# Laying V out by rows behind the weight tiles of the first three stages instead of behind the tiles of U

## What is computed

```python
z = x @ w_in                                   # split among the conv group and the GLA group
mix = concat(conv_mixer(...), gla_mixer(...)) @ w_out
x = layer_norm(ALPHA * x + mix, ln1_g, ln1_b)
# PEER: 8 heads, 128 x 128 product keys, top 16, N_EXPERTS = 16384
q = x @ w_query;  s = q . sub_keys;  ids, gates = top-k of top-k
h = gelu(einsum('td,thkd->thk', x, u_table[ids]))
y = einsum('thk,thkd->td', gates * h, v_table[ids])
x = layer_norm(ALPHA * x + y, ln2_g, ln2_b)
```

## Time and profile before

| | |
|---|---|
| Median of 3 runs | 3986.06 us (3980.82 to 3989.38) |
| The profiled execution's own time | 3983.18 us |
| Its span, first to last instruction | 3981.4 us |
| TensorE busy | 3814.9 us, 96% of the span |
| VectorE, ScalarE, GpSimd busy | 2230.6, 939.1, 1821.2 us |
| Moved by DMA | 751.76 MB |
| Mean granted TensorE clock | 0.972 of full speed |

### The profile page before, as it was taken

The page is one execution under the profiler, slowest core; times in us unless marked ns, Lnnn a source line. Parts: engine busy times, 40 slices in busy tenths (PEclk is TensorE's granted clock), DMA queues, the critical chain, the costliest instruction groups (busy, mean ns, idle before and its releaser), DMA issues.

```text
span 3981.4 us, 64674 instructions
## 1 busy us (share of the span) xinstructions
PE 3814.9 (96%) x26604; PEld 3745.5 (94%) x26604; DVE 2230.6 (56%) x2933; ACT 939.1 (24%) x809; POOL 1821.2 (46%) x895
## 2 busy tenths in 40 slices
PE   8999998797999999999999999999999999999996
PEld 7989998696998999999999999999999999999995
DVE  4876958556799522211111121112687888877877
ACT  3232323223222222222222222222222222222223
POOL 3232322234333487888878885001444444443311
PEclk9999989798999999999999999999999999999998
DMA  3211222353225677777777777665578778777752
GB/s 138 83 64 67 78 75 75 122 222 149 74 95 164 192 206 198 191 200 201 199 193 202 200 192 196 202 200 203 220 280 317 283 290 320 280 295 298 287 213 87
DMA packets 449651, 751.76 MB, mean 189 GB/s; under 512 B 81344, under 2 KB 378752, under 8 KB 386320
## 3 DMA queue, kind: packets, MB, share of 16 engines
q1 hardware_dynamic: 321216, 543.27, 40.4%
q0 software_dynamic: 83968, 134.55, 11.8%
q10 hardware_dynamic: 44368, 72.67, 4.9%
HBM read 677.60 MB, written 207.00 MB: 222 GB/s over the span
## 4 chain that ended last, share of the span: by engine, by line
PE 82%; DVE 13%; DMA 1%; ACT 1%; issue 1%; POOL 1%; SPq 0%; DVEq 0%; ACTq 0%; POOLq 0%
PE ps L554 51%; PE ps L767 27%; DVE yb L1267 2%; DMA wraw<-in_v_t 1%; PE ps L675 1%; PE ps L677 1%; PE ps L630 1%; DVE dist L1155 1%; DVE qe L1186 1%; POOL wl L471 0%; PE ps L660 0%; DVE sif L1379 0%; ACT wh L824 0%; DVE si L1365 0%; DVE oh L1392 0%
## 5 line engine op out<-in xcount | busy, mean ns | idle before, releaser
L554 PE MATMUL ps<-xh,wh 128*128 128x272 f32 x5888 | 1233.7, 291 | 48.4 <-POOL xl L490 21.9
L554 PE MATMUL ps<-xh,wl 128*128 128x272 f32 x5888 | 1225.6, 290 | 0.0
L554 PE MATMUL ps<-xl,wh 128*128 128x272 f32 x5888 | 1221.8, 289 | 0.0
L554 PEld LDWEIGHTS ps<-xh,wh 128*128 128x128 f32 x5888 | 932.4, 190 | 61.2 <-issue 50.2
L513 POOL DMA_INDIRECT g_scratch<-picks,g_col x512 | 869.9, 1699 | 199.5 <-issue 179.5
L554 PEld LDWEIGHTS ps<-xl,wh 128*128 128x128 f32 x5888 | 933.1, 190 | 0.0
L554 PEld LDWEIGHTS ps<-xh,wl 128*128 128x128 f32 x5888 | 926.9, 190 | 0.0
L824 ACT ACTIVATE wh<-wraw 128x2048 fp32r<-128x2048 f32 x328 | 628.4, 1916 | 1122.7 <-PE ps L767 834.7
L1437 DVE TENSOR_TENSOR wl<-wraw,wh 128x2048 fp32r<-128x2048 f32 x114 | 261.5, 2294 | 1099.8 <-ACT wh L824 1005.6
L471 POOL TENSOR_TENSOR wl<-wraw,wh 128x2048 fp32r<-128x2048 f32 x88 | 429.3, 4880 | 824.9 <-ACT wh L824 824.9
L767 PE MATMUL ps<-Wh,wh 128*128 128x416 f32 x2048 | 719.6, 351 | 11.4 <-DVE Wl L1494 7.0
(11 more groups left out here) (234 smaller groups left out, 2558.4 us busy)
## 6 DMA issues: line engine op xcount, KB each, us to landing
wraw<-in_u_t SPq DMA_DIRECT2D x128, 1024.0 KB
v_rows<-in_v_t SPq DMA_DIRECT2D x256, 512.0 KB
wraw<-in_v_t SPq DMA_DIRECT2D x128, 1024.0 KB
wraw<-in_w_in SPq DMA_DIRECT2D x40, 1024.0 KB
g_scratch<-zeros ACTq DMA_DIRECT2D x32, 832.0 KB, 5.0
h_scratch<-hb ACTq DMA_DIRECT2D x64, 416.0 KB
gt<-g_scratch SPq DMA_DIRECT2D x16, 1664.0 KB
hg<-h_scratch SPq DMA_DIRECT2D x16, 1664.0 KB
```

What stands on the lines that cost most here:

```text
L554: ins = mat(out[:, h], w[:, u, k], m[:, k, halves[h]], start=(begin and k == ks[0] and w is wh and m is ah), stop=(end and k == ks[-1] and ...
```

## The change

The two DMAs behind each tile of U are gone. A new loop `stream_rows` issues four of them behind each of 64 earlier tiles: tiles 2 to 37 (`w_in`), 40 to 55 (`w_out`) and 58 to 69 (`w_q`). The waits before the tile loads are the same values as before.

```diff
@@ -377,6 +377,23 @@
+            v_src = v_t.rearrange("(g i) j (d e) c -> g i d j e c", i=EG, d=2)
+            v_dst = v_rows.rearrange("(g e j) (i d c) -> g i d j e c", e=EG, j=P, i=EG, d=2)
+
+            def stream_rows(src, n0, i0, g0, g1):
+
+                s = pairs(src)
+                with sp.Fori(g0, g1) as g:
+                    for q in range(2):
+                        for u in range(2):
+                            i = g * 2 + (q - 2 * g0)
+                            sp.wait_ge(wlo, i * 2 + (n0 + u - 1))
+                            tile(s[bass.ds(i + i0, 1), u].rearrange("o p k c -> (o p) k c"), u)
+                            for m in range(2 * (2 * q + u), 2 * (2 * q + u) + 2):
+                                for d in range(2):
+                                    load(v_dst[bass.ds(g, 1), m, d].rearrange("o j e c -> (o j) e c"),
+                                         v_src[bass.ds(g, 1), m, d].rearrange("o j e c -> (o j) e c"), rows_in)
+
@@ -386,8 +403,9 @@
-            stream(w_in, 2, 1, (NZ + NCV) // 2)
-            stream(w_out, A_OUT, 0, NO // 2)
+            stream_rows(w_in, 2, 1, 0, 9)
+            stream(w_in, 38, 19, 20)
+            stream_rows(w_out, A_OUT, 0, 9, 13)
@@ -395,17 +413,12 @@
-            stream(w_q, A_Q + 2, 1, NQ // 2)
+            stream_rows(w_q, A_Q + 2, 1, 13, 16)
+            stream(w_q, A_Q + 14, 7, NQ // 2)
             us = u_t.rearrange("(g n) p k c -> g n p k c", n=EG)
-            v_src = v_t.rearrange("(g i) j (d e) c -> g i d j e c", i=EG, d=2)
-            v_dst = v_rows.rearrange("(g e j) (i d c) -> g i d j e c", e=EG, j=P, i=EG, d=2)
             def u_tile_in(g, m):
                 a = us[g, m] if isinstance(g, int) else us[bass.ds(g, 1), m].rearrange("o p k c -> (o p) k c")
                 tile(a, m % 2)
-                for d in range(2):
-                    to = v_dst[g, m, d] if isinstance(g, int) else v_dst[bass.ds(g, 1), m, d].rearrange("o j e c -> (o j) e c")
-                    fr = v_src[g, m, d] if isinstance(g, int) else v_src[bass.ds(g, 1), m, d].rearrange("o j e c -> (o j) e c")
-                    load(to, fr, rows_in)
```

## The result

The changed kernel takes 3999.92 us (median of 9 runs, 3991.82 to 4004.92), the kernel before 3983.55 us in the runs beside it (median of 9, 3980.82 to 3993.15). The ratio is 1.0034, 95% interval 1.0024 to 1.0044: slower by about 13.5 us, with 9.6 to 17.5 us as bounds (the two medians themselves lie 16.4 apart, the two profiled executions 15.7). The forecast was 4010 us and +24, in a range of 3981 to 4037. The direction and the place were right; the size was too large by three quarters.

What follows compares the result with a forecast made beforehand. The prediction took TensorE to bound U (gain 0) and DMA to become the bound in w_out: 3983.2 us profiled + 24 = 4007, plus 2.9 for the median of the runs gives 4010 us, range 3981 to 4037.

Steps and rivals of the forecast that it cites:

- Removing the transfers from U gains nothing: In U, TensorE is the bound and hides the 256 transfers, so taking them out gains 0 us.
- w_in and w_q are free: In w_in and w_q, 10.5 us of DMA per tile fit into periods of 12 and 12.6 us: 0 us.
- w_out becomes bound by the DMA engines: In w_out, 15.0 us of DMA per tile exceed TensorE's 12.03 once the lead is used up: +24 us, 50%.
- the marks that were named: In w_out: DMA share near 1.0, tiles at about 15 us, ScalarE's high parts waiting for loads, some 24 us in all.
- Rival 1: In w_out, long DMA runs fill the waits of short ones, demand is nearer 11.9 us: 3986 us, not slower, 25%.
- rival 2: In w_out, loads and zeros fall to the 512 B runs' rate: period up to 17.6 us, +50, 4036 us, 18%.
- Rival 3: In V, another start could take away stalls from where gathers fall in the tile rhythm: -7, 3979 us, 7%.
- the demand of 15.0 us per tile of w_out: DMA time per tile in w_out: 2.9 weight tile, 7.6 four transfers, 4.5 zeros, against TensorE's period of 12.03 us.
- the lower bound: In w_out, all bytes at the zeros' rate, 2.45 us per MB: 11.9 us per tile, under the period, +0.
- tile 48 late by 4 us: In w_out, the first late tile: landing about 842.5 against 838.5; seven tiles 49 to 55 add 2.97 us each.
- the prediction's own formula: In w_out, tile 44+k may land as late as 790.4 + 12.03k us without TensorE losing time.
- The rule of the page: 512 B suffices for line rate: 1.2 us per transfer, 12.2 us per tile in w_out, no loss; the prediction set it aside.

Runs made afterwards that it cites:

- kernel with the 64 alone: Against the kernel before, only the 64 transfers behind w_out's tiles are moved, the other 192 run behind U: 3995.82 us, ratio 1.0024.
- the kernel that fills the pauses: Against the changed kernel, w_out's transfers go where SyncE's queue is empty, before w_out and in the first norm, w_q's behind tiles 60 to 71: 3982.38 us.

## Why the prediction was right, and where it missed

**Removing the transfers from U gains nothing: right.** 256 transfers less in U: +0.0002 (-0.0009 to 0.0013) in the kernel that lays none. TensorE was the bound there and remained it.

**w_in and w_q are free: right.** The two runs without transfers in w_out stand at 0.9997 and 0.9993. The engines have room there, 0.79 in 250 to 350 us, and in 50 to 640 us the view of waits has no wait of ScalarE for a load of w_in, neither before nor after.

**w_out becomes bound by the DMA engines: right**, with the marks that were named: share near 1.0, ScalarE waiting for the loads of eight tiles, 48 to 55, and no wait at the zeros before the norm. Rival 1 (hidden anyway) and rival 2 (the transfers slow the others) both fall by the period of 14.3 us. Rival 3 (a calmer V, -7 us) is not seen in the changed kernel: from V's first product to the end its profile has 1220.0 us, the one before 1217.7. Over all profiles that stretch goes from 1212.4 to 1230.8 us, so V varies by more than the rival is worth, for a reason that no run shows.

**The term that was mis-sized is the demand of 15.0 us per tile of w_out.** It added 2.9 for the tile, 7.6 for four transfers and 4.5 for the zeros, each at its price alone. The period measured is 14.3, or 14.0 where the 64 run alone, and 17.14 with six against 18.8 by the same prices. The queues, read over whole periods, say where the difference lies. First ScalarE's queue (the zeros) over eight periods of the kernel before, 797.39 to 893.61 us; then both queues over seven periods of the changed kernel, 839.08 to 939.26 us:

```profile
q10 hardware_dynamic: 2304, 13.63, 34.7%
```

```profile
q1 hardware_dynamic: 30246, 22.08, 71.8%
q10 hardware_dynamic: 2016, 11.93, 29.0%
```

- *The zeros, 0.3 of the 0.7 us.* A pair takes 0.347 x 96.22 / 8 = 4.2 us of all engines alone, and 0.290 x 100.18 / 7 = 4.15 beside the transfers. The prediction had 4.5 because it divided 37.2 us by 8.3 tiles, while that window had moved 15.18 MB, which is 8.9 pairs of 1.70 MB: 4.2 by bytes. That was a slip in reading a window whose edges cut a burst, and the zeros cost the same beside the transfers as alone.
- *The tile and its four transfers, 0.2.* 0.718 x 100.18 / 7 = 10.3 us, against 10.5.
- *Overlap, 0.1.* The two make 14.4 us of engine time in a period of 14.31, and the share passes 1.00 by as much. The kernel with the 64 alone has the same 14.4 in 13.96, and with six per tile it is 14.1 + 4.1 = 18.2 in 17.14. There the overlap, 1.1 us, is the larger part of the miss and the prices 0.6.

So adding the prices was sound to 3% with four transfers and to 6% with six; the prediction had weighed an overlap only as the lower bound and as rival 1, as a case apart and not as a part of the likeliest one. The price of a transfer alone was right: in the kernel that fills the pauses, SyncE's queue carried nothing else in 965 to 1005 us and ScalarE's nothing at all, with the engines at a share of 0.99:

```profile
q1 hardware_dynamic: 21316, 10.75, 98.2%
```

That is 39.3 us for 10.75 MB, 1.92 us per 0.524 MB.

An excess is a small difference of two large numbers, 15.0 - 12.03 = 2.97 against 14.31 - 12.03 = 2.28, so 5% of the demand became a quarter of the loss per tile. The smaller demand also moved the start: the prediction had tile 48 late by 4 us for TensorE, but its high part came at 839.08, which is 835.9 with the 3.2 us of w_in taken off, and the latest that cost nothing was 838.5. The first that cost TensorE time was tile 50. By tile 55 the lateness was 939.26 - (922.7 + 3.2) = 13.4 us, where 922.7 is 790.4 + 12.03 x 11 of the prediction's own formula; the prediction had 24.8. Of the 11.4 between them, 6.6 arose up to tile 48 and about 4.8 in the seven periods behind. Of the 10.1 us between the forecast of 4010 and the measured 3999.92, 2.5 lie in the base: the median of the kernel before was 3983.55 us in the runs of the comparison and not 3986.06.

**A wait not foreseen:** ScalarE makes the high part of tile 56 before the square of the residual's column, and the load of that tile, of w_q, landed only at 953.2, though nothing needed it before the norm was under way. VectorE got the square late, and the norm began 19.9 us after tile 55's last products (958.2), before 18.8 after them (941.6 in the same way). One microsecond, but it sits on the path, whose chain goes through this load.

**The rule of the page** "DMA: Bandwidth & Descriptors" of the Trainium skill, section Specifications (512 B is enough for line rate) would, by the prediction's estimate with that page's fit (which the page gives for DMAs of GpSimd), have had w_out free with four transfers per tile. The runs disagree: 270 GB/s for the transfers alone at a share of 0.99 (965 to 1005 us of the kernel that fills the pauses), against 408 GB/s for the zeros by the earlier trace rows (15.18 MB in 37.2 us). The transfers differ from the zeros in two things, runs of 512 B and reading and writing DRAM both; no run tells the two apart.

## What to carry to other kernels

Before moving background transfers, add up the DMA time of all queues in the new place, per step of the engine that bounds it. As long as the sum stays below that engine's step the transfers are free, as here with two per tile at a share of 0.90; with three, at 1.03, the lead of the loads still covered it for the 16 tiles; above that the excess of every tile lands on the path. Take the price of a store or load from the bytes that moved in the window, or from whole periods: a window that cuts a burst at its edge gave 4.5 us for 4.2 here. A mean share by stage hides a stage in which another queue already stores: here w_out at 0.61 was the one stage of three that could not take four transfers, and the pauses on both sides of it could take all of them. And where the bounding engine never waits in the old place, moving the transfers out of it has nothing to bring.

## What the runs showed of the hardware

- **A backlog of transfers holds up the sequencer that issues.** Four transfers took SyncE 12.03 us in w_out, 6.4 to 8.3 in w_q (6.4 to 6.6 in its window above, at a share of 0.78), and two took 1.46 in U before. A share near 1 alone doesn't do it: with three per tile, at 1.03 and without a late tile, three took 5.7 to 6.9 us. The chain of the changed kernel runs through these issues in w_out. Since the four took about half as long in w_q, the issuing itself is not what sets 14.3 us. That an earlier issue of the next load would have gained nothing, because it would stand behind the same transfers, is argued and not shown.
- **TensorE's clock fell a little where it waited in every tile.** In w_out of the changed kernel TensorE stands 3.58 us of the window 850 to 900 and the granted clock is 1.00; it stands 7.07 us of 900 to 950, and it is 0.97. All of that fall lies in 930 to 940 us, at 0.83 around a wait of 2.94 us, while the clock stayed at 1.00 after one of 2.85. With six per tile it is 0.93 over 800 to 900 us, so a part of the products ran at the lower level of 1.2 GHz. By the period of 17.14 us that cost nothing, since each high part there waited for its load and not for TensorE, as the prediction had it.

```profile
800.00:900.00 100.00, 85.44 (x632) 84.58 (x631) 42.63 (x26) 14.76 (x12) 28.28 (x7) 0.93 1.06 350
```

- **The head stage has its own scatter.** The changed kernel's profile has TensorE at 0.54 in 284 to 287 us, 16 matmuls in 3 us, where the profile before has 1.00 and 26:

```profile
284.00:287.00 3.00, 3.00 (x16) 3.00 (x16) 3.00 (x1) 0.00 (x0) 3.00 (x1) 0.54 0.00 0
```

```profile
284.00:287.00 3.00, 3.00 (x26) 3.00 (x25) 3.00 (x1) 0.00 (x0) 2.82 (x1) 1.00 0.00 0
```

This place makes 0.7 of the 3.2 us: the chains stand 0.55 us apart at 248 us and 1.25 at 300. Whether places like it make the rest, and the start of w_out between 735 and 748 us over the profiles, is not shown; that start has no order by the number of transfers in w_in. What starts them, and why U takes 1514.2 us in some profiles and 1517.5 in others, stays open.
